# 320 bytes left free in front of the left operands of a two-block transformer kernel on one core

## What is computed

```python
def reference(x, ...):
    x = first_block(x, c, w_ada, ..., w_in, ..., w_out, w_ff1, w_ff2)
    return second_block(x, mem_2, ..., w_in_2, ..., w_out_2, w_cq_2, w_ckv_2, w_co_2, w_up_2, ..., w_down_2)

# in both blocks, around the token mixers:
proj = rmsnorm(x) @ w_in                     # [256, 2048] @ [2048, 8208] and [2048, 6168]
y = jnp.concatenate(mixers(proj), -1) @ w_out
x = x + gate * norm(y)
y = act(norm(x) @ w_ff1) @ w_ff2             # hidden width 8192; in the second block 5504, gated
```

## Time and profile before

| | us |
|---|---|
| time, median of 3 runs (lowest, highest) | 3149.5 (3148.46, 3151.79) |
| time of the profiled execution | 3149.72 |
| its span, first to last instruction | 3147.9 |
| PE busy | 2777.4 (88%) |
| PEld busy | 2297.6 (73%) |
| DVE busy | 1861.4 (59%) |
| ACT busy | 1245.1 (40%) |
| mean granted TensorE clock | 0.936 |

### The profile page before, as it was taken

One profiled execution on the slowest core, in us unless ns is written; L12 is line 12 of the kernel. 1 busy time (PEld: TensorE's weight loads), 2 busy tenths in 40 slices (PEclk: granted clock), 3 DMA queues, 4 the chain that ended last, 5 costly groups with the idle time before them and its releaser, 6 DMA issues.

```text
span 3147.9 us, 33041 instructions
## 1 busy us (share of the span) xinstructions
PE 2777.4 (88%) x12695; PEld 2297.6 (73%) x12695; DVE 1861.4 (59%) x2115; ACT 1245.1 (40%) x1538; POOL 55.4 (2%) x89
## 2 busy tenths in 40 slices
PE   2399998677969999999979998869879999999986
PEld 1288886576758888888858887758668888887874
DVE  7679765866575555555674443474554655556454
ACT  0144445432434444444434443333444444444432
POOL 2000000000000000000000000000000000000000
PEclk9899998988989999999989997559999999999998
DMA  9487886024645555555645553015345555555552
GB/s 352 184 282 277 292 282 213 27 81 174 240 174 187 187 186 183 183 182 186 244 182 174 191 196 104 1 53 192 116 148 186 177 180 192 173 193 168 174 166 73
DMA packets 146237, 563.29 MB, mean 179 GB/s; under 512 B 13816, under 2 KB 18023, under 8 KB 137808
## 3 DMA queue, kind: packets, MB, share of 16 engines
q1 hardware_dynamic: 141568, 538.28, 49.8%
q0 software_dynamic: 4560, 23.53, 2.1%
HBM read 557.32 MB, written 4.46 MB: 178 GB/s over the span
## 4 chain that ended last, share of the span: by engine, by line
PE 79%; DVE 12%; ACT 3%; issue 3%; DMA 2%; POOL 1%; DVEq 0%; ACTq 0%; POOLq 0%
PE banks L365 24%; PE banks L367 23%; PE banks L366 23%; PE banks L423 2%; DMA raw_weights<-in_w_ada 2%; ACT weights_high L313 1%; DVE weights_low L325 1%; DVE mod_in L345 1%; PE banks L944 1%; PE banks L937 1%; DVE lhs_low L436 1%; DVE y_rows L1195 1%; POOL small L510 1%; DVE x_rows L408 1%; PE banks L1438 1%
## 5 line engine op out<-in xcount | busy, mean ns | idle before, releaser
L325 DVE TENSOR_TENSOR weights_low<-raw_weights,weights_high 128x1024 fp32r<-128x1024 f32 (+4 forms) x894 | 1025.6, 1154 | 1005.2 <-ACT weights_high L313 1004.0
L313 ACT ACTIVATE weights_high<-raw_weights 128x1024 fp32r<-128x1024 f32 (+4 forms) x894 | 890.6, 1001 | 1262.9 <-PE banks L367 1209.4
L365 PE MATMUL banks<-weights_high,lhs_high 128*128 128x512 f32 (+3 forms) x2560 | 1012.8, 396 | 30.3 <-DVE lhs_low L436 14.8
L367 PE MATMUL banks<-weights_high,lhs_low 128*128 128x512 f32 (+3 forms) x2560 | 999.1, 390 | 0.0
L366 PE MATMUL banks<-weights_low,lhs_high 128*128 128x512 f32 (+3 forms) x2560 | 998.3, 390 | 0.0
L365 PEld LDWEIGHTS banks<-weights_high,lhs_high 128*128 128x128 f32 x2560 | 491.8, 192 | 132.2 <-DVE lhs_low L436 17.0
L367 PEld LDWEIGHTS banks<-weights_high,lhs_low 128*128 128x128 f32 x2560 | 490.9, 192 | 103.9
L366 PEld LDWEIGHTS banks<-weights_low,lhs_high 128*128 128x128 f32 x2560 | 491.7, 192 | 94.9
L365 PE MATMUL banks<-weights_high,hid_high 128*128 128x512 f32 x856 | 339.5, 397 | 18.2 <-DVE hid_low L1825 9.7
L366 PE MATMUL banks<-weights_low,hid_high 128*128 128x512 f32 x856 | 336.9, 394 | 0.0
L367 PE MATMUL banks<-weights_high,hid_low 128*128 128x512 f32 x856 | 336.0, 393 | 0.0
(11 more groups left out here) (356 smaller groups left out, 1798.1 us busy)
## 6 DMA issues: line engine op xcount, KB each, us to landing
raw_weights<-in_w_ff SPq DMA_DIRECT2D x128, 1024.0 KB, 5.0
raw_weights<-in_w_in SPq DMA_DIRECT2D x112, 1024.0 KB, 5.4
raw_weights<-in_w_ada SPq DMA_DIRECT2D x96, 1024.0 KB, 5.1
raw_weights<-in_w_up SPq DMA_DIRECT2D x80, 1024.0 KB, 4.9
raw_weights<-in_w_down SPq DMA_DIRECT2D x42, 1024.0 KB, 5.0
raw_weights<-in_w_out SPq DMA_DIRECT2D x32, 1024.0 KB, 5.1
raw_weights<-in_w_ckv SPq DMA_DIRECT2D x8, 1024.0 KB, 4.9
raw_weights<-in_w_up SPq DMA_DIRECT2D x16, 384.0 KB, 3.3
```

The costliest lines, as they stand in the source:

```text
L313: act.activation(WHI[:, u % SPN, 0:c.width], RAW[:, n % RAWN, k % 2, 0:c.width], ACT.Copy).then_inc(S("high_made"), 1)
L325: dve.tensor_tensor(WLO[:, u % SPN, 0:c.width], RAW[:, n % RAWN, k % 2, 0:c.width], WHI[:, u % SPN, 0:c.width].bitcast(F32), ALU.subtract) ...
L365: nc.tensor.matmul(o, lh[:, k, tk], hi, start=(k == 0), stop=False)
L367: mm = nc.tensor.matmul(o, ll[:, k, tk], hi, start=False, stop=(k == c.kn - 1))
```

## The change

One tensor of 80 float32 per partition, 320 bytes, is declared behind `small`. Nothing reads or writes it.

```diff
         GATES = psb("gates", [128, 10, 16])
         SM = psb("small", [128, 256])
+        psb("spacing", [128, 80])
         IDENT, ONES, UPPER, AFTER, NEG_T, CAUSAL = (CF[:, j, :] for j in range(6))
         LT = [("lhs_high", [128, KT, T], F32R), ("lhs_low", [128, KT, T], F32R)]
```

## The result

| | before | after |
|---|---|---|
| time, median (lowest, highest) of 4 runs, us | 3149.49 (3148.46, 3151.79) | 3129.26 (3125.04, 3134.88) |
| profiled execution, its span, us | 3149.72, 3147.9 | 3125.04, 3123.2 |
| mean granted clock of that execution | 0.936 | 0.939 |
| pitch of the 512-column matmuls at the full clock, ns: on `lhs_*`, on `hid_*` | 229.01, 229.14 | 227.12, 226.88 |

The kernel became faster: the ratio of the times is 0.9936, with a 95% interval of 0.9919 to 0.9953.

The account below looks back on a forecast made before the run. The prediction took the pitch of 9864 long PE matmuls as the bound. Its four terms (load, streaming, other engines, DMAs) were each 0, with ends at 60 us either way, giving 3149.5 us, no change, range 3130 to 3170 us.

Parts of the forecast that it names:

- What bounds the kernel: Lines 365 to 367: the pitch of 9864 matmuls, 0.2290 us each, sets the pace; 1 ns is worth 9.9 us.
- First, the load: Loading left operands, median 188 ns, has some 40 ns to spare beside the matmul ahead; priced at 0 us.
- Second, the streaming: Distance modulo 2048 from the streamed block to the block loaded beside it changes; taken as 0 us, ends 59 us either way.
- equal rows of lines 423 and 944: Transposes (423) and matmuls (944) from differently placed blocks: durations agreed within 1 to 2 ns, taken as evidence of no effect.
- Third: Other engines on moved tensors, DVE with 378 us of the chain: taken as 0, ends 0.5 us either way.
- Fourth: DMAs into the moved region, hidden but for a remainder: taken as 0, ends 0.4 us either way.
- The granted clock: It follows what PE does; as no gap of PE changes, its course was left as it is.
- the pitch falls: Long matmuls: matching places give back part of 15.2 ns a pitch; 59 us gain, 3090 us, far end 3000; chance 0.15.
- the pitch grows: Long matmuls: load and stream starting at the same place modulo 512 meet more often; 59 us cost, 3209 us; chance 0.13.
- the change doesn't do what it says: Left operands miss a true multiple of 2048 by 128 bytes, so time stays 3149.5 us; 0.22 within no change's 0.72.
- The range: 3130 to 3170 us, 2 ns a pitch or 20 us either way, given 0.81.
- The test that I wrote down: Full-clock pitch leaving 0.2284 to 0.2296 us proves the forecast wrong; the loads' median tells whether they slowed too.

Follow-up runs that it names:

- e9: Matmul loop alone, other engines resting, sections moving single operands or changing sizes; with the same two left blocks throughout, 226.8 ns a pitch at distance 0, 233.3 at 64.
- e4: Kernel before plus a 64-byte tensor ahead of all tensors, so that everything moves by 64 bytes: 3150.77 us, ratio 1.0005 to before.
- e5: Kernel before plus a 256-byte tensor behind `small`, instead of the change's 320 bytes: 3149.71 us, ratio 1.0003 to before.
- e2: Kernel before plus a 128-byte tensor behind `small`, instead of the change's 320 bytes: 3184.8 us, ratio 1.0116 to before.
- e3: Kernel before plus a 192-byte tensor behind `small`, putting left operands on a true multiple of 2048: 3179.0 us, ratio 1.0095 to before.
- e6: Changed kernel plus a 64-byte tensor ahead of all tensors, moving left and streamed operands together: 3130.67 us, ratio 0.9933 to before.
- e8: Matmul loop alone, nothing of the reference computed, other engines resting, distance varied by section: 226.6 ns a pitch at 0, 233.3 at 64, 229.0 at 192.

## Why the prediction was wrong, step by step

**What bounds the kernel** held. The pitch of the 9864 matmuls sets the pace, and 1 ns of it is worth nearly 9.9 us: 2.0 ns gave 20 us.

**"First, the load"**: held in what it says, the median load still takes 188 ns. Its last clause, that a longer load would vanish in 40 ns, wasn't tested.

**"Second, the streaming"** is the step that failed. It named the distance between left and streamed operands, which is what counts (whether by the block that is loaded beside the stream is open, by e9), and said rightly that steps of 512 do nothing. Then it took 0 for what lies within 512, by the equal rows of lines 423 and 944; measured were 1.89 ns a pitch on `lhs_*` and 2.26 on `hid_*`, 19.6 us. These rows can't show the price. The prediction calls them "of the right type", and they are not: they are plain float32 with 128 streamed columns, and e9 has plain float32 at 429.2 ns at each of three distances, and fp32r with 128 columns at 111.3 and 111.7. Equal rows of another form were taken as evidence that an effect is absent, where they could only say that it is absent in that form. A hint stood in the stream itself: a shortest duration of 387 ns under a median of 393, and 15 ns a pitch that aren't columns. I used these 6 ns as an end of the range and not as a clue.

**"Third" and "Fourth"**, DVE and DMAs: 0 held. DVE's busy time went from 1861.4 to 1860.1 us, and e4 and e5, which move tensors and keep the distance, are within 0.05% of before.

**The granted clock** I left as it was. Over the four runs of after it is 0.939, 0.938, 0.937 and 0.935, and the times are 3125.04, 3127.87, 3130.66 and 3134.88 us, the lower the clock the longer. The profiled execution of after is the fastest of them. Set matmul by matmul beside that of before, 19.2 of its 24.7 us lie in starts within 0.26 us of the one ahead in both; 3.1 us lie in 22 of the long matmuls that had a pitch at the lower clock, over 0.4 us, in one execution and at the full clock in the other (19 of them in before); the last 2.4 us lie elsewhere. So two single executions would have overstated what the pitch gains.

**The rival "the pitch falls"** was given 0.15 and was right that the places have a price, of which this change gives part back. That they have to match is not so in general: 16, 36 and 40 bytes are as good as 0, and with 256 streamed columns 64 is better. Its price, 6 ns or 59 us, was three times too large, since the shortest matmuls aren't what all come to: all come to a middle value. The excess didn't go: 227 - 214 = 13 of the 15 ns stay.

**The rival "the pitch grows"** is true of other distances: e2 and e3 have its sign and two thirds of its 6 ns. The Trainium skill (SBUF — State Buffer, "Who interferes with whom"), by which it fell, gives TensorE a read port for the streamed operand and an independent one for the loaded operand. The runs contradict what the prediction drew from it, that the distance of the two operands costs nothing: with PE alone at work the pitch goes from 226.7 to 235.0 ns by it. Whether the two ports have a part in that, no run shows.

**The rival "the change doesn't do what it says"** has the fact right, the operands stand 128 bytes over a true multiple of 2048, and the conclusion wrong: what counts is the distance to the streamed tensors. At the true multiple, e3, the kernel is slower.

**The range** was drawn at 2 ns a pitch, a third of the way to each rival's end; the true size was 2.0 ns, and 3129.26 falls 0.7 us outside. The test that I wrote down, a pitch outside 0.2284 to 0.2296 us with the load's own median unmoved, is what came out. By itself it could not tell the distance from the place of the left operands; e3, e4 and e6 did.

## What to carry to other kernels

Where a long stream of fp32r matmuls sets the pace, count the pitch from starts in a stretch without pauses, and let left and streamed operands begin at the same place modulo 256 bytes (found for 128 loaded and 512 streamed columns; with 256 streamed or 96 loaded columns another distance was better, and bf16 and plain float32 didn't care). What matters is the distance of the two, which any small tensor that is declared between them changes, by 2.7% of the pitch from after to e2; a round address is worth nothing by itself. And a row of another type or size that shows no effect is no bound on the effect.

## What the runs showed of the hardware that I had not expected

- The pitch of fp32r matmuls depends on where two operands of the same engine lie in different tensors: up to 8.3 ns come on top of 226.7, by the distance modulo 256 bytes, with no other engine at work (e8, e9).
- It goes by no simple rule: at distances of 0 and 16, 36 and 40 bytes 226.7 ns, at 32 and 64 233.3, at 44 230.2, at 192 229.0, at 28 235.0.
- In the stretches shown the single pitches come in fixed patterns. In after they settle, behind the first five (228 to 236 ns), into 226, 227, 227; in e2 they are 231 and 236 in turn, to 1 ns, and in e3 229 and 238.
- There is no such price at the lower clock. In e2, whose pitch at the full clock is 6.2 ns over that of after, 7 pitches take 167.54 - 164.55 = 2.99 us (2.98 in after); 7 times 6.2 ns would be 0.04 us more. Over the whole traces the long matmuls' pitches at the lower clock (those between 415 and 445 ns) have a mean of 426.4 ns in before (38 of them), 426.6 in after (22) and 426.2 in e2 (36).

```profile
164.55 0.63 PE L367 MATMUL banks<-weights_low,lhs_high 128*128 128x512 f32 x1
...
167.54 0.63 PE L368 MATMUL banks<-weights_high,lhs_low 128*128 128x512 f32 x1
```

- bf16 runs at 215.9 ns for 512 columns, which agrees with the 215.7 ns of the Trainium skill (TensorE: Matmul & The Clock Gate, "Wait — 56ns, not 53.3ns?"); fp32r with 512 columns never came below 226.6 in any section.

Open are which two reads meet, since neither the loaded block beside the streaming nor a matmul's own pair accounts for e9; why the price depends on the distance as it does; and where the 10.8 ns come from that fp32r has over bf16 at its best distance.
